# Seven block products for eight in the second gate and up products of a hybrid decoder layer

## The reference, cut to what matters

```python
x = x + 0.5 * swiglu(rmsnorm(x, ffn1_norm), w_gate1, w_up1, w_down1)
h = rmsnorm(x, mix_norm)                    # mLSTM and differential attention on h
x = x + merged @ w_out
x = x + 0.5 * swiglu(rmsnorm(x, ffn2_norm), w_gate2, w_up2, w_down2)
def rmsnorm(x, g): return x * rsqrt(mean(x * x, axis=-1) + 1e-6) * g
def swiglu(x, w_gate, w_up, w_down): return (silu(x @ w_gate) * (x @ w_up)) @ w_down
```

## Time and profile before

| | |
|---|---|
| median of 3 runs | 1680.73 us (1680.59 to 1681.77) |
| span of the profiled execution, first to last instruction | 1676.3 us |
| the profiled execution's own time | not listed apart from its span; the median is 4.4 us above the span |
| granted PE clock, mean of the span | 0.995 |
| PE / VectorE / ScalarE busy | 98% / 46% / 33% |
| HBM | 97 GB/s over the span |

### The profile page before, as it was taken

One profiled execution on the slowest core, in us unless ns is written; L12 is line 12 of the kernel. 1 busy time (PEld: TensorE's weight loads), 2 busy tenths in 40 slices (PEclk: granted clock), 3 DMA queues, 4 the chain that ended last, 5 costly groups with the idle time before them and its releaser, 6 DMA issues.

```text
span 1676.3 us, 30583 instructions
## 1 busy us (share of the span) xinstructions
PE 1641.3 (98%) x12808; PEld 1559.7 (93%) x12808; DVE 764.4 (46%) x1152; ACT 557.5 (33%) x848; POOL 4.5 (0%) x20
## 2 busy tenths in 40 slices
...
DMA packets 246788, 164.08 MB, mean 98 GB/s; under 512 B 8350, under 2 KB 229779, under 8 KB 246714
## 3 DMA queue, kind: packets, MB, share of 16 engines
...
## 4 chain that ended last, share of the span: by engine, by line
PE 92%; DVE 3%; ACT 2%; DMA 2%; issue 1%; SPq 1%; DVEq 0%; ACTq 0%
PE ps L411 73%; PE ps L823 3%; PE ps L1041 2%; PE ps L1005 1%; PE ps L395 1%; PE ps L1241 1%; PE ps L1192 1%; PE ps L903 1%; PE ps L1311 1%; PE ps L1090 1%; DVE small L2423 1%; PE ps L1402 1%; PE ps L1355 1%; PE ps L1430 1%; PE ps L1238 1%
## 5 line engine op out<-in xcount | busy, mean ns | idle before, releaser
L411 PE MATMUL ps<-xn_hi,w_hi 128*128 128x272 f32 (+1 forms) x2192 | 635.4, 290 | 4.0 <-DVE w_lo L383 3.4
L411 PE MATMUL ps<-xn_hi,w_lo 128*128 128x272 f32 (+1 forms) x2192 | 637.5, 291 | 0.0
L411 PE MATMUL ps<-xn_lo,w_hi 128*128 128x272 f32 (+1 forms) x2192 | 634.5, 289 | 0.0
L379 ACT ACTIVATE w_hi<-raw 128x1024 fp32r<-128x1024 f32 (+1 forms) x198 | 220.1, 1112 | 820.8 <-PE ps L411 813.6
L411 PEld LDWEIGHTS ps<-xn_hi,w_hi 128*128 128x128 f32 x2192 | 413.7, 189 | 5.1 <-DVE w_lo L383 3.8
L411 PEld LDWEIGHTS ps<-xn_hi,w_lo 128*128 128x128 f32 x2192 | 413.4, 189 | 0.0
L411 PEld LDWEIGHTS ps<-xn_lo,w_hi 128*128 128x128 f32 x2192 | 412.5, 188 | 0.0
L383 DVE TENSOR_TENSOR w_lo<-raw,w_hi 128x1024 fp32r<-128x1024 f32 (+1 forms) x198 | 255.2, 1289 | 210.9 <-ACT w_hi L379 210.5
L411 PE MATMUL ps<-h_lo,w_hi 128*128 128x280 f32 (+1 forms) x660 | 191.9, 291 | 0.0
L411 PE MATMUL ps<-h_hi,w_lo 128*128 128x280 f32 (+1 forms) x660 | 191.9, 291 | 0.0
L411 PE MATMUL ps<-h_hi,w_hi 128*128 128x280 f32 (+1 forms) x660 | 191.9, 291 | 0.0
...
## 6 DMA issues: line engine op xcount, KB each, us to landing
raw<-in_w_in SPq DMA_DIRECT2D x55, 512.0 KB, 3.8
raw<-in_ffn_w_gate SPq DMA_DIRECT2D x44, 512.0 KB, 3.8
raw<-in_ffn_w_up SPq DMA_DIRECT2D x44, 512.0 KB, 3.8
...
pages<-in_cache_k SPq DMA_DIRECT2D x16, 512.0 KB, 4.5
pages<-in_cache_v SPq DMA_DIRECT2D x16, 512.0 KB, 5.4
```

The lines of the kernel that those rows point to most:

```text
L379: act.activation(w_hi[s][:, 0:p.nk, :], raw[s][:, 0:p.nk, :], ACT.Copy).then_inc(hi_done[s], 1)
L411: mm = pe.matmul(ps[:, bank + half, 0:p.half], w[s][:, k, :], x[:, k0 + k, cols], start=first and k == 0 and a == 0, stop=last and k == p. ...
```

## The change

The gate panel and the up panel of one j are taken as one 256 x 1024 matrix. Its weights are cut into four blocks (gate and up; even and odd tiles of 128 along k), the activations into four (even and odd tiles; early and late 272 tokens). One level of Strassen's scheme, in the form with sums that build on each other, computes the product from seven block products instead of eight. A block product is 4 k pairs x 3 = 12 matmuls of 128 x 272 (`seventh`). The weight side needs a11, a12, a22 as they are and four sums, s1 to s4; the activation side three blocks as they are and four sums. All are split into hi and lo.

- **Activations** (once): `scaled_tile` writes the scaled tiles to W4, VectorE forms sums in T4, both are split to XH and XL, seven blocks per pair of tiles. xn_hi and xn_lo go.
- **Weights**: `raw_panel` loads a gate panel to rawg (one buffer) and an up panel to rawu (two buffers), two DMAs of 256 KB each. VectorE forms S31 (two sums), S2 and S4 (into rawu). ScalarE splits G (a11, a12), S31, S2 and U (a22, s4); G, S31 and S2 have one buffer each, U two.
- **Products**: the order on PE is p1, p2, p4 of the panel before, p6, the s1 product, p3 of the panel before, p7. Three partial sums (after p1, p6 and p7) are copied out of PSUM by ScalarE while the bank goes on accumulating (`first_sum`, `second_sum`, `third_sum`, semaphore part7). VectorE joins them: `gate_1`, `gate_2` (an add, then a multiplication by rn, which waits for the add), `up_sum`, and `hidden_1`, `hidden_2`, which write h32 unsplit. Each works on 272 tokens.
- **h** is split into h_hi and h_lo at the border to the down product: `h_split` and `h_rest`, 22 tiles of 544 each, after the last panel.
- **Around it**: PE waits for evac[1] before w_out's first product, and p_wo uses banks 4 to 7. rms stands behind first_sum(0). All loops of the stage are written out. `more` and `after` are waits on semaphores used before, offset by what was spent.

The diff, cut to its core, with eight columns of indentation taken off:

```diff
+BC = H2
+XH = at("XH", [128, DT // 2, 7, BC], f32r, xn0)
+S31 = at("S31", [128, 2, 4, 128], f32, xn0 + 28 * BC * 4)
...
+rawg = at("rawg", [128, 4, 2, 128], f32, slots)
+rawu = [at(f"rawu{q}", [128, 4, 2, 128], f32, slots + 4096 + 4096 * q) for q in range(2)]
+S2_hi, S2_lo = at("S2_hi", [128, 4, 128], f32r, slots + 12288), at("S2_lo", [128, 4, 128], f32r, slots + 14336)
...
+    n = 0 if p is up2 else p.n
...
-    return p in (p_om, p_b)
+    return p in (p_om, p_b, up2)
...
+PRODUCT7 = [(n, 0) for n in ("p1", "p2", "p6", "p7")]
+    PRODUCT7 += [("p1", j), ("p2", j), ("p4", j - 1), ("p6", j), ("p3", j - 1), ("p7", j)]
...
-    stream(up2)
+    def raw_panel(p, j):
+        wg, wu = (w[:, 128 * j:128 * j + 128].rearrange("(k two p) n -> p k two n", two=2, p=128) for w in p.w)
+        if j == 0:
+            for s in range(2):
+                sp.wait_ge(lo_done[s], p.before)
+        else:
+            after(sp, lo7, LO7, "g", j - 1)
+            after(sp, sum7, SUM7, "s4", j - 1)
+        for two in range(2):
+            sp.dma_start(rawg[:, :, two, :], wg[:, :, two, :]).then_inc(in_g7.sem, 16)
+        if j == 1:
+            for s in range(2):
+                sp.wait_ge(mm_done[s], p.before)
+        elif j >= 2:
+            after(sp, lo7, LO7, "u", j - 2)
+        for two in range(2):
+            sp.dma_start(rawu[j % 2][:, :, two, :], wu[:, :, 1 - two, :]).then_inc(in_u7[j % 2].sem, 16)
+    for j in range(FT):
+        raw_panel(up2, j)
...
     pe.wait_ge(evac[0], p_wo.ev0)
+    pe.wait_ge(evac[1], p_wo.ev0)
     pe.wait_ge(lo_done[0], p_wo.before + 1)
...
-    pe.wait_ge(evac[1], p_wo.ev0)
-    product(pe, p_wo, 0, 1, 2, m_hi, m_lo)
-    pair(p_wo, ((m_hi, m_lo), (m_hi, m_lo)), first=1)
+    product(pe, p_wo, 0, 1, 6, m_hi, m_lo)
+    pair(p_wo, ((m_hi, m_lo), (m_hi, m_lo)), first=1, bank=4)
...
-    first(up2, 2)
-    up(up2)
+    def seventh(w_of, block, bank, pairs=range(DT // 2), first=False):
+        for k in pairs:
+            for a, (w, x) in enumerate(((0, XH), (0, XL), (1, XH))):
+                mm = pe.matmul(ps[:, bank, 0:n7], w_of(w)[:, k], x[:, k, block, 0:n7],
+                               start=first and k == 0 and a == 0, stop=k == DT // 2 - 1 and a == 2,
+                               skip_group_check=True)
+        return mm
...
+    def rest_of(j):
+        c = 4 * (j % 2)
+        after(pe, lo7, LO7, "u", j)
+        after(pe, part7, PART7, "r3", j)
+        seventh(a22(j % 2), 5, c).then_inc(product7.sem, 1)
+        def last():
+            after(pe, hidden7, HIDDEN7, "u2", j)
+            seventh(s4(j % 2), 1, c + 1).then_inc(product7.sem, 1)
+        return last
+    def strassen(j):
+        c = 4 * (j % 2)
+        after(pe, lo7, LO7, "g", j)
+        if j >= 2:
+            after(pe, hidden7, HIDDEN7, "h1", j - 2)
+        if j >= 1:
+            seventh(a11, 0, c, first=True).then_inc(product7.sem, 1)
+            if j >= 2:
+                after(pe, gate7, GATE7, "g1", j - 2)
+            seventh(a12, 2, c + 2, first=True).then_inc(product7.sem, 1)
+            last = rest_of(j - 1)
+        else:
+            early, rest = range(DT // 2 - 1), range(DT // 2 - 1, DT // 2)
+            for k in early:
+                more(pe, xl_done, 3 * k + 1)
+            seventh(a11, 0, c, early, first=True)
+            seventh(a12, 2, c + 2, early, first=True)
+            norm(2, up2, (3, 7))
+            more(pe, xl_done, 3 * (DT // 2) - 2)
+            seventh(a11, 0, c, rest).then_inc(product7.sem, 1)
+            seventh(a12, 2, c + 2, rest).then_inc(product7.sem, 1)
+            more(pe, xl_done, 3 * (DT // 2))
+        after(pe, lo7, LO7, "s2", j)
+        after(pe, part7, PART7, "r1", j)
+        seventh(s2, 6, c).then_inc(product7.sem, 1)
+        after(pe, lo7, LO7, "s31", j)
+        if j >= 2:
+            after(pe, gate7, GATE7, "g2", j - 2)
+        seventh(s1, 3, c + 1, first=True)
+        if j >= 1:
+            last()
+        after(pe, part7, PART7, "r2", j)
+        seventh(s3, 4, c).then_inc(product7.sem, 1)
+    for j in range(FT):
+        strassen(j)
+    rest_of(FT - 1)()
...
+    def scaled_tile(i):
+        copy(W4[:, 2 * (i % 2):2 * (i % 2) + 2, 0:n7], tok(X[:, i, :], up2),
+             scale=gcol[:, G_FFN2 + i:G_FFN2 + i + 1]).then_inc(w4_ready.sem, 1)
+        square(2, i, c7)
+    def operands_hi(k):
+        more(act, w4_ready, 2 * k + 2)
+        copy(XH[:, k, 0:3, 0:n7], W4[:, 1:4, 0:n7]).then_inc(xh_done.sem, 1)
+        more(act, t4_ready, k + 1)
+        copy(XH[:, k, 3:6, 0:n7], T4[:, 0:3, 0:n7]).then_inc(xh_done.sem, 1)
+        copy(XH[:, k, 6, 0:n7], T4[:, 3, 0:n7], scale=-1.0).then_inc(xh_done.sem, 1)
...
+            elif s == 1:
+                g_split(0)
+                s31_split(0)
             act.wait_ge(evac[s], j + p_wo.ev0 + 1)
-            tile(2, 2 * j + s, NMETA)
+            if j >= 1:
+                more(act, xl_done, 3 * j)
+            scaled_tile(2 * j + s)
+        operands_hi(j)
-    split_hi(act, up2, 0, 1)
-    rms(2, up2)
-    gated(up2, ACT.Silu, h_hi)
+    s2_split(0)
...
+    first_sum(0)
+    rms(2, up2, 4)
+    act.activation(small[0:1, 60:61], con[0:1, 0:1], ACT.Silu)
+    u_split(0)
+    for j in range(FT):
+        if j >= 1:
+            first_sum(j)
+        if j + 1 < FT:
+            g_split(j + 1)
+        gate(j, "g1", late7)
+        second_sum(j)
+        if j + 1 < FT:
+            s2_split(j + 1)
+            u_split(j + 1)
+        if j >= 1:
+            gate(j - 1, "g2", early7)
+        third_sum(j)
+        if j + 1 < FT:
+            s31_split(j + 1)
+    after(act, product7, PRODUCT7, "p3", FT - 2)
+    split_hi(act, down2, 0, 0)
+    gate(FT - 1, "g2", early7)
+    for k in range(KD):
+        h_split(k)
+    split_hi(act, down2, 0, 1)
+    for k in range(KD, FT):
+        h_split(k)
...
+    def sums_31(j):
+        more(v, in_g7, 32 * (j + 1))
+        more(v, in_u7[j % 2], 32 * (j // 2 + 1))
+        v.tensor_tensor(S31[:, 0], rawg[:, :, 0, :], rawu[j % 2][:, :, 1, :], ALU.add)
+        v.tensor_tensor(S31[:, 1], rawu[j % 2][:, :, 0, :], rawu[j % 2][:, :, 1, :], ALU.add).then_inc(sum7.sem, 1)
...
+    def gate_sum(j, name, bank, part, product_, r, cols):
+        after(v, part7, PART7, part, j)
+        after(v, product7, PRODUCT7, product_, j)
+        g = t2[j % 2][:, cols]
+        v.tensor_tensor(g, ps[:, 4 * (j % 2) + bank, 0:n7], r, ALU.add).then_inc(gate7.sem, 1)
+        after(v, gate7, GATE7, name, j)
+        v.tensor_tensor(g, g, rn[:, cols], ALU.mult).then_inc(norm7.sem, 1)
...
+            if j == DT // 2 - 1 and s == 0:
+                sums_31(0)
+                sum_2(0)
+                g_rest(0)
+                s31_rest(0)
+        operands(j)
+    v.wait_ge(rn_ready, 3)
+    v.tensor_scalar(rh[:, c7:], rn[:, c7:], 0.5, None, ALU.mult)
...
+    for j in range(FT):
+        if j >= 1:
+            up_sum(j - 1)
+        else:
+            sum_4(0)
+            s2_rest(0)
+        u_rest(j)
+        if j >= 1:
+            s31_rest(j)
+        if j >= 2:
+            hidden_2(j - 2)
+        gate_1(j)
+        if j + 1 < FT:
+            sums_31(j + 1)
+        if j >= 1:
+            hidden_1(j - 1)
+        if j + 1 < FT:
+            sum_2(j + 1)
+            g_rest(j + 1)
+            sum_4(j + 1)
+            s2_rest(j + 1)
+        if j >= 1:
+            gate_2(j - 1)
+    up_sum(FT - 1)
+    hidden_2(FT - 2)
+    split_lo(v, down2, 0, 0)
+    hidden_1(FT - 1)
+    gate_2(FT - 1)
+    hidden_2(FT - 1)
+    for k in range(KD):
+        h_rest(k)
+    split_lo(v, down2, 0, 1)
+    for k in range(KD, FT):
+        h_rest(k)
```

More of the change, by code:

```diff
@@ L14 @@
+from collections import namedtuple
 from contextlib import ExitStack
@@ L918, in down_last, with pair @@
                 last_down(p)
-            def pair(p, xs_, first=0):
+            def pair(p, xs_, first=0, bank=0):
                 def body(j, _q, _jn):
@@ new lines, in third_sum, with gate @@
+            def third_sum(j):
+                after(act, product7, PRODUCT7, "p7", j)
+                if j >= 2:
+                    after(act, hidden7, HIDDEN7, "h2", j - 2)
+                c = H2 * (j % 2)
+                copy(acc[:, c:c + n7], ps[:, 4 * (j % 2), 0:n7]).then_inc(part7.sem, 1)
+            def gate(j, name, cols):
+                after(act, norm7, GATE7, name, j)
+                act.activation(t2[j % 2][:, cols], t2[j % 2][:, cols], ACT.Silu).then_inc(silu7.sem, 1)
+            early7, late7 = slice(c7, c7 + n7), slice(c7 + n7, T)
@@ new lines, in sums_31, with sum_2 @@
+            def sums_31(j):
[3 more added lines that the diff above has]
+                v.tensor_tensor(S31[:, 1], rawu[j % 2][:, :, 0, :], rawu[j % 2][:, :, 1, :], ALU.add).then_inc(sum7.sem, 1)
+            def sum_2(j):
+                after(v, sum7, SUM7, "s31", j)
+                v.tensor_tensor(S2[:, :, :], S31[:, 1], rawg[:, :, 0, :], ALU.add).then_inc(sum7.sem, 1)
@@ new lines, in sum_4, with g_rest, s31_rest @@
+            def sum_4(j):
```

(10 more changed lines are left out.)

182 lines of the change are left out of this document (162 added, 20 removed).

## The result

| | before | after |
|---|---|---|
| median | 1680.73 us | 1666.78 us (1664.32 to 1669.94, 4 runs) |
| span of the profiled execution | 1676.3 us | 1662.5 us |
| matmuls of PE | 12808 | 12544 |

The ratio is 0.9921, 95% interval 0.9906 to 0.9935: faster by 0.8%. The forecast was 1668.6, range 1661 to 1679. The profiled execution is the fastest of the four (1664.3 us), so its trace shows the changed kernel at its best.

What follows compares the result with a forecast made beforehand. PE's matmuls were taken to bound the kernel. The terms -33.2 + 1.8 + 11.7 + 0.7 + 5.9 + 1.0 = -12.1 took the time from 1680.73 to 1668.6 us, range 1661 to 1679.

Steps and rivals of the forecast that it cites:

- Removed, -33.2: Gate and up loop: 8 products of 12 matmuls become 7 per panel pair, 22 x 12 x 0.1258 = -33.2 us.
- Why the loop held: Panel loop: VectorE's 9.3 us and ScalarE's 5.9 fit below PE's 10.55, smallest cover 2.3, so no added cost.
- the 1.1 us until third_sum: Panel loop: VectorE laid out as idle for 1.1 us between gate_2 behind p3 and the next third_sum.
- Each us of VectorE over 10.55 costs 21: Panel loop: if the cover goes, each us of VectorE work over 10.55 a panel costs 21 us.
- the load was put at 5.2: Raw panel loads: last of four 256 KB loads lands in 5.2 us behind sum_4's end, ends 3.8 and 8.0.
- rival C: Raw loads and sum_4 form a ring, binding when landing passes 6.4; at 8.0, +32.5 us, time 1701; chance 0.12.
- p_wo starts later, +1.8: Start of p_wo: PE waits for evac[1] before the first w_out product, not after it, costing +1.8 us.
- The stage's start, +11.7: Gate and up stage's start: 12.5 us lost until panel 1's p1, less 0.84 lost before, +11.7; ends 9 and 15.
- the -9 of the rule: Stage's start: with the skill's 1.38 us drain per table switch, chain 2.8 longer, sum -9 instead of -12.
- The end: Stage's end: last p4 waits for third_sum, +0.7; splitting h before the down products, +5.9, ends 4.5 and 8.
- The clock, +1.0: PE's clock falls after idle stretches at the stage's borders; one fall may lie on the path, +1.0 (0 to 5).
- rival A: Borders cost more: clock falls at each idle stretch and in panel 1's p1, p2; +4 to +9, about 1675; chance 0.14.

Runs made afterwards that it cites:

- e5_dve1: Changed kernel with one more VectorE instruction a panel (about 0.6 us), ahead of g_rest; ratio to before 0.9942.
- e7_cut: Changed kernel with p5's matmuls left out (12 a panel), so hidden is not the reference's; 1657.9 us, ratio to before 0.9845.
- e13_upfirst: e9_cutswap with the raw up half asked for once its buffer is free, only the gate half waiting for sum_4; 1638.8 us, ratio to before 0.9756.
- e9_cutswap: Changed kernel with p5 left out and ScalarE's third_sum ahead of gate_2's Silu; 1658.3 us, ratio to before 0.9881.
- e1_evac: Changed kernel with PE's wait for evac[1] put back behind w_out's first product; 1662.1 us, ratio to before 0.9902.
- e10_warm: Changed kernel with 102 matmuls whose results nobody reads filling five of PE's idle gaps; 1667.6 us, ratio to before 0.9925.

## Why the prediction was right, step by step

**Removed, -33.2: right.** 264 matmuls less, at a pitch of 0.1253 to 0.1258 with no wait in the loop. That the loop was PE's stands by e5_dve1 to e7_cut too: it has neighbours at 10.0 us a panel, and PE's 10.53 is over them.

**Why the loop held: right in the outcome, partly wrong in the reason.** VectorE's chain was put at 9.3 and is 9.19 (e13_upfirst). The term for scalar_tensor_tensor was 0.50 and is 0.44. But the prediction called the 1.1 us until third_sum idle, and held that VectorE could fill it. It is a link of a ring (gate_2, Silu, third_sum, up_sum), and the time that can be filled is what PE's 10.53 leaves over 10.0. "Each us of VectorE over 10.55 costs 21" holds for work beyond that half us, not beyond the 1.2 that VectorE's own 9.3 seemed to leave. And the load was put at 5.2. From the first issue until VectorE has the last load it is 6.0 at the mean of e9_cutswap's panels (5.6 to 6.4), with 6.4 the point at which rival C's ring binds: a cover of 0.4 instead of 1.2. In the changed kernel VectorE did wait for a load three times in the loop, 2.1 us in all, at 5.7, 6.6 and 7.0 behind the first issue, which G_lo's cover kept from PE. Rival C was wrong, and nearer than the forecast made it.

The two instructions beside one another overlap as the earlier trace rows had it: the 15 instructions of a panel last 10.2 us by their rows and take 9.19. The Trainium skill, VectorE: DVE Perf Modes, The DRAIN you can't avoid, says that the next operation does not start until the pipe is empty, and goes on that one which is not held starts earlier. The trace agrees with the second part, which the prediction left out; by the first alone a panel would take over 10.2.

**p_wo starts later, +1.8: right.** 1.84 in the trace after, none in e1_evac.

**The stage's start, +11.7: right, 0.9 too small.** The steps at s, forecast and measured: norm 5.35 and 5.63, rn 11.3 and 11.63, p6 13.1 and 13.41, p7 18.4 and 18.72, p1 of panel 1 20.8 and 21.73. (p7 is no proof of its step: second_sum, for which it was to wait, is done at 18.3, and p7 follows straight behind p5, which the lower clock had drawn out to 18.7.) About 0.3 is there from the norm on and is carried along; the rest is u's landing, forecast 5.2 behind sum_4's end and measured 5.8. The two Ln and Exp table loads (ScalarE's timeline, as the earlier trace rows) are on the path as predicted:

```profile
1268.80 1.28 ACT L1705 ACT_TABLE_LOAD   x1
1270.09 0.71 ACT L1705 ACTIVATE rn<-ps,con 128x544 f32<-128x544 f32 x1
1270.82 1.28 ACT L1708 ACT_TABLE_LOAD   x1
1272.12 0.66 ACT L1708 ACTIVATE rn<-rn 128x544 f32<-128x544 f32 x1
```

Each activation follows its load by 0.01 to 0.02. So the row decided rightly for -12 over the -9 of the rule (ScalarE: Activation LUTs, What ACT_TABLE_LOAD costs, in the Trainium skill), whose drain of 1.38 a switch has no place here.

**The end: right.** third_sum 0.74 for 0.7, from one matmul's start to the next less a pitch of 0.125 (the row's 0.58 counts from the modelled end). The h border 3.1 and, in the down products, 2.6 more than before: 5.7 for 5.9.

**The clock, +1.0: about the mean of what it costs, and nothing in the profiled execution.** There it fell to 0.50 twice, at 1272.7 and 1511.7. The first stretch lies under the wait for the load, as forecast, and e10_warm takes it away without a gain; the second lies mostly under the wait for h tiles. In five of nine executions with this start it fell under the norm instead and cost p1 of panel 1 about 1.4. In e5_dve1 it fell a second time, in p1 and p2 of panel 1, rival A's very place, which cost 1.5. So A's mechanism is there; its price of 4 to 9 is not. That the changed kernel's own other three executions, 1.0 to 5.6 us above the profiled one, had such falls fits this and is not shown.

**The sum**: -33.1 + 1.8 + 12.6 + 0.7 + 5.7 = -12.3 in place of -12.1 (of which +1.0 was the clock). The spans differ by 13.8. Of the other 1.5, 0.9 is the stretch ahead of p_b's end, which neither kernel changes, and 0.7 the pitch, 0.1258 before and 0.1254 after over the 1788 matmuls from p1 of panel 1 on; against that w_out's matmuls take 0.3 longer. What is left is 0.2. The 4.4 us between span and median stayed (4.3 after), but not as a fixed cost: an execution's own time is 1.7 to 1.8 above its span wherever both are listed, and the rest is that both profiled executions were faster than their medians, by luck by about as much.
